# Seven products for the values of two dilated groups, tokens halved by residue, with evenly spread additions and transposed powers in the delta stage

## The chip, the cores and the metric

The kernel is one launch on one NeuronCore of a Trainium2 chip. The metric is device time in microseconds (us), the median of several executions. All matrices are float32. A float32 matmul shows in the profile as two MATMUL records, each with a LDWEIGHTS record of its own; a transpose through the identity matrix shows as one.

## The reference, cut to what matters

Two layers over 512 tokens of width 1024: an attention mixer with a mixture of experts, then a gated delta-rule mixer with a mixture of experts. Two places matter here.

- Attention: `qkv = h @ w_in` for three groups of 16 heads of 64 features. Group 0 attends to a window of 128 positions; groups 1 and 2 are dilated by 4, so that a query of residue r (its position modulo 4) sees only keys and values of residue r. q and k are rotated (`q * cos + swapped(q) * sin`), then come a softmax over all three groups together, the weighted sum of values, and the output projection.
- Delta rule: per head and per block of 128 tokens the inverse of a unit triangular matrix, `(I - A)^-1`, is needed.

## The kernel before

The program is a row of stages with a barrier of all engines between them: first (the modulated input `c.hT`, [128, 8 slices of the width, 512 tokens]), attention, experts, delta, experts.

**Attention.** Four turns (quads), of four heads each. A quad takes nine chunks of projection weights (256 features each, 1 MB) through a ring of three slots, in the order q0, k0, v0, q1, k1, q2, k2, v1, v2. SyncE (SP) asks for chunk n+3 as soon as chunk n is done with: after the halves of a q or k were swapped (`swapped`, L553), or after the value matmuls (`v_done`).

Each of the six q and k chunks (numbered s = 0 to 5) is projected by seven products in place of eight (`product_1` to `product_7`, Strassen's way in Winograd's form): features, the contraction and the tokens are halved, the tokens into the first 256 and the last 256 (`h11` to `h22`, L483). The weights stand still and 256 tokens move, so a product is 4 matmuls of 256 columns. Four of the products take token sums `t1` to `t4`, made once by VectorE in `c.x` at the start; the others take `h11`, `h21`, `h22` as they lie in `c.hT`. GpSimd makes four weight sums for each chunk (`add_up`, L694). Partial results are copied by ScalarE (`keep_m1`, `keep_u2`, `keep_u3`, `lay_21`, `keep_m5`) and joined by VectorE (`join`, L743), which lets TensorE overwrite the banks. VectorE then rotates (`rot`, `swp`) and writes q, k1 and k2 in the order of residues, through a strided output (L774, L778), k0 in the order of tokens (L776).

The values of group 0 are plain matmuls of 256 columns with 128 neighbouring tokens standing still (L912). The values of groups 1 and 2 (`PAIRED`, L907) go together: the 128 tokens of one residue stand still, `c.hT[:, kk, t:SEQ:RES]`, read with a step of four elements, and 512 features move, 256 of each group: 4 residues x 8 slices = 32 matmuls of 512 columns a quad. Four banks' worth of results are copied by ScalarE.

Beside this the stage builds the modulation rows for later (`AdaRows`): 24 weight tiles a quad, loaded by GpSimd's queue (L210, L213) into three slots and added up by VectorE (`ada.add`, L230). After chunk s's rotation begins, 2 additions are made, and after its end a further 2, 8, 2, 2, 0, 0 (`BETWEEN`, `BEHIND`, L541). The load of addition j waits for addition j-3, and GpSimd takes its work in order: the sums of chunk s+1, then the loads up to the additions behind chunk s. Matmuls with ones (`ada.total`, L246) and `ada.finish` (L255) end the rows. Behind the last value matmul TensorE starts the next quad's `product_1`; then scores, softmax, transposes and weighted values of the quad follow in eight steps.

**Delta.** Four turns of two heads. For each the powers of a nilpotent P and of its transpose Q are built (L2717 on): TensorE makes both P' = QP and Q' = PQ by four matmuls each (`each`, L2643), ScalarE copies both out (L2450, L2452), and `P E` is added to E by VectorE (L2620). Then three levels of links follow.

Of the kernel before, what the change touches and what calls it, by code (L numbers as in the profile page):

```python
# [274 lines left out]
def first_stage(nc, c, A, ring):  # L275
# [40 lines left out]
    with nc.Block() as block:  # L316
# [32 lines left out]
        def _(dve):  # L349
# [8 lines left out]
            ch.do(nc.vector.tensor_scalar(ang[:], pos[:], freq[:, 0:1], None, ALU.mult))  # L358
# [68 lines left out]
def attention_stage(nc, c, A, ada_rows, ring):  # L427
# [10 lines left out]
    VALS = 6  # L438
# [31 lines left out]
    ada = AdaRows(nc, c, st, A, (1, 2), ada_rows, 3, gate=True)  # L470
# [12 lines left out]
    h11, h12, h21, h22 = [c.hT[:, a * KH:(a + 1) * KH, b * SH:(b + 1) * SH] for a in range(2) for b in range(2)]  # L483
    toks = c.x[:].rearrange("p t n -> p (t n)").rearrange("p (m k s) -> p m k s", m=4, k=KH)
# [20 lines left out]

    sem = st.sem
    chain_done, second_done, third_done = sem("chain_done"), sem("second_done"), sem("third_done")
# [10 lines left out]
    VC = 2  # L518
# [22 lines left out]
    BETWEEN, BEHIND = 2, (2, 8, 2, 2, 0, 0)  # L541

    with nc.Block() as block:
        @block.sync
        def _(sp):
# [18 lines left out]
            def turn(i, following):  # L564
                ada.load_bias(sp, i)
                for n, (g, s) in enumerate(chunks):
                    if s < 2:
                        swapped(i, subs.index(n))
                    else:
                        sp.wait_ge(v_done, VALS * i + (2 if n < PAIRED else VALS))  # L570
# [23 lines left out]
        def _(act):  # L594
            act.sem_inc(chain_kept, 8)
            act.sem_inc(v_free, VC)
# [29 lines left out]
            def quad(i, following):  # L626
                b = 0
                for n, (g, s) in enumerate(chunks):
                    if s < 2:
# [8 lines left out]
                        continue  # L638
                    for _ in range(0 if n > PAIRED else 4 if n == PAIRED else 2):
                        act.wait_ge(v_done, VALS * i + b + 1)  # L640
                        bank = tp[b % 2][:].rearrange("p b q -> p (b q)").rearrange("p (a f) -> p a f", f=QF)
                        if n >= PAIRED:
                            nc.scalar.copy(v[:, 1:3, b - 2, :], bank).then_inc(v_free, 1)
                        else:
                            nc.scalar.copy(v[:, g, 2 * b:2 * b + 2, :], bank).then_inc(v_free, 1)
                        b += 1
# [45 lines left out]
        def _(pool):  # L692
# [16 lines left out]

            with pool.Fori(0, QUADS) as i:  # L710
                add_up(i, 0)
                j = 0
                for s in range(NSUB):
                    if s + 1 < NSUB:
                        add_up(i, s + 1)
                    for _ in range(min(BETWEEN + BEHIND[s] + (ada.slots if s == 0 else 0), ada.steps - j)):
                        ada.load(pool, i, j)
                        j += 1
                assert j == ada.steps

        @block.vector
        def _(dve):
# [17 lines left out]
            for i in range(QUADS):  # L740
# [12 lines left out]
                j = 0  # L753
                for s in range(NSUB):
# [7 lines left out]
                    for _ in range(min(BETWEEN, ada.steps - j)):  # L762
                        ada.add(dve, i, j)
                        j += 1
# [3 lines left out]
                    for pair in range(2):  # L768
                        if pair == 0:
                            ch.sync()  # L770
                        a = rot[:, pair].rearrange("p (j r) -> p j r", r=RES)
                        b = swp[:, pair].rearrange("p (j r) -> p j r", r=RES)
                        if keys == 0:
                            ins = nc.vector.tensor_tensor(q[:, g, pair].rearrange("p (r j) -> p j r", r=RES), a, b, ALU.add)  # L774
                        elif g == 0:
                            ins = nc.vector.tensor_tensor(k0[:, pair, P:P + SEQ], rot[:, pair], swp[:, pair], ALU.add)  # L776
                        else:
                            ins = nc.vector.tensor_tensor(k[:, g - 1, pair].rearrange("p (r j) -> p j r", r=RES), a, b, ALU.add)  # L778
                        ins.then_inc(rot_done, 1)
                    dve.wait_ge(rot_done, NROT * i + 2 * s + 4)  # L780
                    for _ in range(BEHIND[s]):
                        ada.add(dve, i, j)
                        j += 1
                assert j == ada.steps
                ada.finish(dve, i, 0, side, 1)
                ada.finish(dve, i, 2, gate_side, 2)
                ada.finish(dve, i, 1, side, 3)
# [34 lines left out]
        def _(pe):  # L822
# [7 lines left out]
            def times(out, left, right, kks, done, start=False):  # L830
                for kk in kks:
                    last = nc.tensor.matmul(out, left[:, kk], right[:, kk], start=start and kk == 0, stop=kk == KH - 1,
                                            skip_group_check=True)
                if kks[-1] == KH - 1:
                    last.then_inc(done, 1)

# [35 lines left out]
            def quad(i, following):  # L872
                b = 0
                for n, (g, s) in enumerate(chunks):
                    if s < 2:
                        u = subs.index(n)
                        if u == 0:
                            pe.wait_ge(sm_ready, UNITS * i + 2)
                            product_5(i, 0)
                            product_2(i, 0)  # L880
# [13 lines left out]
                    if n > PAIRED:  # L894
                        continue
                    pe.wait_ge(w_in[n % SLOTS], 16 * (CH // SLOTS) * i + 16 * (n // SLOTS + 1))
                    if n == PAIRED:
                        pe.wait_ge(w_in[(n + 1) % SLOTS], 16 * (CH // SLOTS) * i + 16 * ((n + 1) // SLOTS + 1))
                    else:
                        pe.wait_ge(pT_ready, UNITS * i + 2)  # L900
                    for _ in range(4 if n == PAIRED else 2):
                        pe.wait_ge(v_free, VALS * i + b + 1)
                        bank = tp[b % 2][:].rearrange("p b q -> p (b q)")
                        if n == PAIRED:
                            t = b - 2
                            for kk in range(KT):
                                last = nc.tensor.matmul(bank.rearrange("p (a f) -> p a f", f=QF), c.hT[:, kk, t:SEQ:RES],  # L907
                                                        w[:, PAIRED % SLOTS:PAIRED % SLOTS + 2, kk], start=kk == 0, stop=kk == KT - 1)
                        else:
                            for t in range(2 * b, 2 * b + 2):  # L910
                                for kk in range(KT):
                                    last = nc.tensor.matmul(bank[:, t % 2 * QF:(t % 2 + 1) * QF], c.hT[:, kk, t * P:(t + 1) * P],  # L912
                                                            w[:, n % SLOTS, kk], start=kk == 0, stop=kk == KT - 1)
                        last.then_inc(v_done, 1)
                        b += 1
                        if b == VALS - 2:
                            pe.wait_ge(ada.ready, ada.readies * i + 2)
                            ada.total(pe, i, 2, gate_side)
                pe.wait_ge(ada.ready, ada.readies * i + 3)
                ada.total(pe, i, 1, side)  # L920
                if following:
# [57 lines left out]
                for step in range(PAIRS + 3):  # L979
                    if step == 0:  # L980
                        pe.wait_ge(rot_done, NROT * (i + 1) + 2)
                        pe.wait_ge(ada.ready, ada.readies * (i + 1))
                        scores(0)
# [6 lines left out]
                    if step == 0:  # L990
                        pe.wait_ge(v_free, VALS * (i + 1) + VC)
# [9 lines left out]
            product_1(0, 0)  # L1001
            pe.wait_ge(toks_ready, 2)
            product_6(0, 0)
            pe.wait_ge(toks_ready, 4)
            product_7(0, 0)
# [1248 lines left out]
def delta_stage(nc, c, A, ada_rows, ring):  # L2254
# [75 lines left out]
    pw_ready = [sem(f"pw_ready{n}") for n in range(3)]  # L2330
    e_done = [sem(f"e_done{n}") for n in range(6)]
# [27 lines left out]
    with nc.Block() as block:  # L2359
# [24 lines left out]
        def _(act):  # L2384
# [23 lines left out]
            with act.Fori(0, TURNS) as i:  # L2408
# [36 lines left out]
                for s, (pd, qd) in enumerate(((P1, Q1), (P0, Q0), (P1, None))):  # L2445
                    for h in range(HP):
                        act.wait_ge(pw_done[s], 2 * i + h + 1)
                        if s == 1:
                            act.wait_ge(E_first, 2 * i + h + 1)
                        last = nc.scalar.copy(pd[h][:], ps[h][1][:])  # L2450
                        if qd is not None:
                            last = nc.scalar.copy(qd[h][:], ps[h][2][:])  # L2452
# [370 lines left out]
```

## Time and profile before

| | us |
|---|---|
| median of 3 runs (2622.71 to 2629.01) | 2624.84 |
| the profiled execution's own time | 2624.83 |
| its span, first to last instruction | 2623.1 |
| TensorE busy in the span | 2456.6 (94%) |
| VectorE, ScalarE, GpSimd busy | 1209.0, 588.0, 490.8 |

The mean granted clock of TensorE is 0.983 of full speed. TensorE is busy nearly everywhere, so the table says which engine to look at, not what a change is worth.

### The profile page before, as it was taken

To read this page: it belongs to the slowest core of one execution; us is meant where nothing else is said; L and a number is where in the kernel's file an instruction comes from. 1 tells how busy PE (TensorE), PEld (TensorE's weight loads), DVE (VectorE), ACT (ScalarE), POOL (GpSimd) and SP (SyncE) were. 2 spreads that over 40 slices of the span, in tenths; PEclk is the share of its full clock that TensorE was granted. 3 is DMA by queue.
4 is the path that set the end of the run, shared out by engine and by line. 5 is a ranking of instruction groups with operands and counts; after the bars stand their busy time and mean duration, and the time that the engine had idled before them with its cause. 6 is when DMAs were issued, how large, how long until landed. Compare 5 with 4: busy or idle time off the path is not lost. (4 is left out here: it accounts for less than half of the span.)

```text
span 2623.1 us, 38415 instructions
## 1 busy us (share of the span) xinstructions
PE 2456.6 (94%) x14213; PEld 1443.2 (55%) x14214; DVE 1209.0 (46%) x2562; ACT 588.0 (22%) x1357; POOL 490.8 (19%) x488
## 2 busy tenths in 40 slices
PE   5999999998999999999998999999899999999996
PEld 3878787776854333333334658576764433333332
DVE  3846566574444333332245544635443443333326
ACT  1131131413111111111113443334211111111111
POOL 2504224240001111111100212222001111111110
PEclk9999999999999999999998999999999999999998
DMA  7726354363468999999964131221629999999967
GB/s 255 208 72 193 113 153 121 106 184 119 194 231 331 388 421 418 410 420 398 418 252 169 52 91 53 68 72 40 232 102 340 364 418 420 402 420 414 396 272 292
DMA packets 173625, 657.36 MB, mean 251 GB/s; under 512 B 25300, under 2 KB 87100, under 8 KB 118296
## 3 DMA queue, kind: packets, MB, share of 16 engines
q1 hardware_dynamic: 117936, 409.57, 40.8%
q10 hardware_dynamic: 20280, 136.27, 12.9%
q0 software_dynamic: 35248, 109.36, 12.0%
q8 instruction: 103, 1.69, 0.3%
q14 instruction: 58, 0.48, 0.1%
HBM read 616.27 MB, written 53.52 MB: 255 GB/s over the span
## 5 line engine op out<-in xcount | busy, mean ns | idle before, releaser
L1724 DVE TENSOR_SCALAR core_oT<-moe_tx,moe_by,moe_plus 128x128 f32<-128x128 f32 x360 | 123.0, 404 | 543.8 <-PE moe_tx L1989 543.7
L2028 PE MATMUL moe_py<-weights_w,moe_hT 128*32 128x512 f32 (+2 forms) x1296 | 312.7, 596 | 0.9 <-ACT moe_hT L1444 0.9
L2014 PE MATMUL moe_ph<-weights_w,core_oT 128*32 128x512 f32 (+2 forms) x1216 | 303.6, 615 | 2.5 <-issue 2.5
L2014 PE MATMUL moe_pr<-weights_w,core_oT 128*64 128x512 f32 (+2 forms) x864 | 274.2, 601 | 10.5 <-DMA core_ring<-in_expert_w_dram 6.3
L1523 POOL DMA_INDIRECT y_rows<-moe_ysb,moe_yidx x90 | 102.2, 1136 | 929.7 <-DVE moe_idx L1716 563.1
L1444 ACT COPY moe_hT<-moe_th 128x256 f32<-128x256 f32 x90 | 33.6, 373 | 917.1 <-PE moe_th L1977 917.1
L2657 PE MATMUL gdn_pj<-core_hT,core_ring 128*128 128x512 f32 x512 | 226.3, 596 | 5.2 <-ACTq L2391 5.2
L2657 PEld LDWEIGHTS gdn_pj<-core_hT,core_ring 128*128 128x128 f32 x512 | 96.8, 191 | 122.1 <-issue 122.1
L2014 PEld LDWEIGHTS moe_pr<-weights_w,core_oT 128*64 128x64 f32 (+2 forms) x864 | 92.0, 141 | 125.5 <-issue 124.9
L2028 PEld LDWEIGHTS moe_py<-weights_w,moe_hT 128*32 128x32 f32 (+2 forms) x1296 | 92.4, 128 | 120.6 <-issue 113.3
L2028 PE MATMUL moe_py<-core_ring,moe_hT 128*32 128x512 f32 (+2 forms) x416 | 145.3, 596 | 2.6 <-DVE moe_ysb L1861 2.6
L2014 PE MATMUL moe_ph<-core_ring,core_oT 128*32 128x512 f32 (+2 forms) x512 | 145.0, 602 | 1.8 <-issue 1.8
L1416 ACT ACTIVATE core_oT<-moe_tx,moe_plus,moe_by 128x128 f32<-128x128 f32 x360 | 135.6, 456 | 46.8 <-PE moe_tx L1989 46.8
L1861 DVE SCALAR_TENSOR_TENSOR moe_ysb<-core_ada,moe_py 128x512 f32<-128x512 f32 x180 | 115.6, 683 | 54.5 <-PE moe_py L2028 54.0
L2014 PEld LDWEIGHTS moe_ph<-weights_w,core_oT 128*32 128x32 f32 (+2 forms) x1216 | 85.4, 121 | 93.4 <-issue 92.9
L2014 PE MATMUL moe_ph<-core_hT,core_oT 128*32 128x512 f32 (+1 forms) x416 | 127.2, 594 | 1.9 <-issue 1.9
L1519 POOL DMA_INDIRECT core_oT<-h_rows,moe_idx x90 | 91.4, 1015 | 135.7 <-DVE moe_yidx L1720 63.6
L907 PE MATMUL attn_tp<-core_ring,core_hT 128*128 128x512 f32 x256 | 111.2, 592 | 0.0
L2014 PE MATMUL moe_pr<-core_hT,core_oT 128*64 128x512 f32 (+2 forms) x224 | 99.1, 595 | 0.0
L1989 PE MATMUL moe_tx<-core_ident,core_oT 128*128 128x128 f32 x720 | 95.2, 275 | 0.0
L907 PEld LDWEIGHTS attn_tp<-core_ring,core_hT 128*128 128x128 f32 x256 | 78.6, 309 | 29.7
L2014 PE MATMUL moe_pr<-core_ring,core_oT 128*64 128x512 f32 (+1 forms) x192 | 89.8, 623 | 0.0
(455 smaller groups left out, 4173.4 us busy)
## 6 DMA issues: line engine op xcount, KB each, us to landing
weights_w<-in_expert_w_dram SPq DMA_DIRECT2D x160, 1024.0 KB, 14.9
weights_w<-in_expert_w_dram ACTq DMA_DIRECT2D x92, 1024.0 KB, 10.5
core_ring<-in_expert_w_dram SPq DMA_DIRECT2D x54, 1024.0 KB, 14.7
core_hT<-in_expert_w_dram SPq DMA_DIRECT2D x48, 1024.0 KB, 13.9
core_ring<-in_attn_w_in_dram SPq DMA_DIRECT2D x36, 1024.0 KB, 6.3
weights_w<-y_rows SPq DMA_DIRECT2D x32, 1024.0 KB, 13.3
core_ring<-in_expert_w_dram ACTq DMA_DIRECT2D x30, 1024.0 KB, 10.1
attn_ada_w<-in_ada_w_dram POOLq DMA_DIRECT2D x64, 384.0 KB, 4.2
```

What stands on the lines that cost most here:

```text
L907: last = nc.tensor.matmul(bank.rearrange("p (a f) -> p a f", f=QF), c.hT[:, kk, t:SEQ:RES], w[:, PAIRED % SLOTS:PAIRED % SLOTS + 2, kk], s ...
L1416: last = nc.scalar.activation(xT[:, b, k], tx[0][:, k], ACT.Identity, scale=by[:, k:k + 1], bias=plus[:, k:k + 1])
L1444: nc.scalar.copy(hT2[:, p % 2], th[:]).then_inc(hT_ready, 1)
L1519: pool.indirect_dma_start(xg[:, b], None, h_rows, bass.IndirectOffsetOnAxis(ap=idx[:, b:b + 1], axis=0), bounds_check=SEQ - 1, oob_is_err= ...
L1523: pool.indirect_dma_start(y_rows, bass.IndirectOffsetOnAxis(ap=yidx[:, s:s + 1], axis=0), ysb[:, b], None, bounds_check=SEQ * TOPK - 1, oo ...
L1724: last = nc.vector.tensor_scalar(xT[:, b, k], tx[1][:, k - 4], by[:, k:k + 1], plus[:, k:k + 1], ALU.mult, ALU.add)
L1861: return nc.vector.scalar_tensor_tensor(out=out, in0=c.ada[:, 2, at], scalar=1.0, in1=in_, op0=ALU.add, op1=ALU.mult)
L1989: last = nc.tensor.transpose(tx[n][:, k], xg[:, b, 4 * n + k::KT], c.ident[:])
L2014: last = nc.tensor.matmul(ph[p % 2][at, :], xT[:, p % 2, k, at], w13[ew.up_place(n)[0]][:, :, k], start=k == 0, stop=k == KT - 1)
L2028: last = nc.tensor.matmul(py[n][at, :], hT2[:, p % 2, k, at], w2[ew.down_place(m)[0]][:, k, half(n)], start=k == 0, stop=k == 1)
L2657: last = nc.tensor.matmul(pj[m % 2][:], w[:, slot, k, m % 2 * P:(m % 2 + 1) * P], c.hT[:, k], start=k == 0, stop=k == KT - 1)
```

## The change

- The tokens are halved by residue: `h11` to `h22` and the sums `t1` to `t4` are residues 0 and 1, or 2 and 3. A half of `c.hT` is thus read with a step of four elements. The rotation tables are built in residue order too.
- q, k1 and k2 are now written densely; k0 is written with a step.
- The values of groups 1 and 2 become seven products: tokens by residue, the contraction, and group 1 against group 2. A product is 2 residues x 4 slices = 8 matmuls with 128 tokens standing still and 256 features moving. Four new weight sums a quad, each [128, 1024], are made by GpSimd (`add_up_values`), behind the sums of the last q or k chunk.
- Each chunk has four additions, two between and two behind, with four slots; the loads behind chunk s go only as far as its additions between.
- At the very start `product_2` is put ahead of `product_6`, and `product_7` waits for three token sums, not four.
- In the delta stage Q' is no longer a product: P' is copied out and transposed.

```diff
-    h11, h12, h21, h22 = [c.hT[:, a * KH:(a + 1) * KH, b * SH:(b + 1) * SH] ...]
+    by_residue = c.hT[:].rearrange("p k (j r) -> p k r j", r=RES)
+    h11, h12, h21, h22 = [by_residue[:, a * KH:(a + 1) * KH, b * RES // 2:(b + 1) * RES // 2] ...]
...
+    v11, v12, v21, v22 = [w[:, v_slots[b], a * KH:(a + 1) * KH] for b in range(2) for a in range(2)]
-    BETWEEN, BEHIND = 2, (2, 8, 2, 2, 0, 0)
+    ADDS = ada.steps // NSUB
...  (GpSimd)
+            def add_up_values(i):
+                for n in (PAIRED, PAIRED + 1):
+                    pool.wait_ge(w_in[n % SLOTS], ...)
+                nc.gpsimd.tensor_tensor(vs1, v21, v22, ALU.add).then_inc(v_sums, 1)
+                nc.gpsimd.tensor_tensor(vs2, vs1, v11, ALU.subtract).then_inc(v_sums, 1)
+                nc.gpsimd.tensor_tensor(vs3, v11, v21, ALU.subtract).then_inc(v_sums, 1)
+                nc.gpsimd.tensor_tensor(vs4, v12, vs2, ALU.subtract).then_inc(v_sums, 1)
...
                 for s in range(NSUB):
                     if s + 1 < NSUB:
                         add_up(i, s + 1)
-                    for _ in range(min(BETWEEN + BEHIND[s] + (ada.slots if s == 0 else 0), ada.steps - j)):
+                    else:
+                        add_up_values(i)
+                    far = ADDS * s + ADDS // 2 + ada.slots
+                    for j in range(ada.slots if s == 0 else far - ADDS, min(far, ada.steps)):
                         ada.load(pool, i, j)
...  (VectorE, behind the six chunks)
                 ada.finish(dve, i, 0, side, 1)
+                nc.vector.tensor_tensor(v[:, 1, 0:2], v[:, 1, 0:2], v_second, ALU.add).then_inc(v_joined, 1)
+                ada.finish(dve, i, 1, side, 2)
+                nc.vector.tensor_tensor(v[:, 1, 2:4], v[:, 1, 2:4], v_third, ALU.add).then_inc(v_joined, 1)
+                nc.vector.tensor_tensor(v[:, 2, 2:4], v[:, 2, 2:4], v_m5, ALU.add).then_inc(v_joined, 1)
+                ada.finish(dve, i, 2, gate_side, 3)
...  (TensorE, in place of the paired values)
+            def v_times(out, left, right, done, start=False):
+                for t in range(2):
+                    for kk in range(KH):
+                        last = nc.tensor.matmul(out[:, t], left[:, kk, t], right[:, kk], ...)
+                v_times(v_chain, h11, v11, v_chain_done, start=True)
+                v_times(v_second, h21, v12, v_second_done, start=True)
+                pe.wait_ge(v_sums, SUMS * i + 2)
+                v_times(v_chain, t2, vs2, v_chain_done)
+                v_times(v_third, t1, vs1, v_third_done, start=True)
+                pe.wait_ge(ada.ready, ada.readies * i + 2)
+                ada.total(pe, i, 1, side)
+                v_times(v_chain, t3, vs3, v_chain_done)
+                v_times(v_third, h22, vs4, v_third_done)
+                v_times(v_chain, t4, v22, v_chain_done)
+                pe.wait_ge(ada.ready, ada.readies * i + 4)
+                ada.total(pe, i, 2, gate_side)
...  (delta stage, TensorE)
-                    each(ps[h][1], lambda t: Q0[h][:, t], lambda t: P0[h][:, t])
-                    each(ps[h][2], lambda t: P0[h][:, t], lambda t: Q0[h][:, t]).then_inc(pw_done[0], 1)
+                    each(ps[h][1], lambda t: Q0[h][:, t], lambda t: P0[h][:, t]).then_inc(pw_done[0], 1)
...
                         if s < 2:
-                            last = each(ps[h][1], lambda t: q[h][:, t], lambda t: p[h][:, t])
+                            turn(ps[h][2], p[h], q_done[s])
                         if s == 0:
-                            each(ps[h][2], lambda t: p[h][:, t], lambda t: q[h][:, t]).then_inc(pw_done[1], 1)
                             pe.wait_ge(qk_ready, n)
                         each(ps[h][0], lambda t: p[h][:, t], lambda t: e[h][:, t]).then_inc(e_done[s], 1)
+                    if s < 2:
+                        for h in range(HP):
+                            pe.wait_ge(q_ready[s], 2 * i + h + 1)
+                            each(ps[h][1], lambda t: q[h][:, t], lambda t: p[h][:, t]).then_inc(pw_done[s + 1], 1)
```

## Rows read from the trace of the kernel before

**Rows 1.** Windows: stretch, its length, busy us (records) per engine, clock, DMA.
```profile
42.00:650.00 608.00, 586.60 (x3688) 470.40 (x3688) 380.17 (x657) 149.79 (x369) 195.41 (x192) 1.00 0.46 140
1425.00:1534.00 109.00, 108.58 (x561) 73.89 (x560) 55.80 (x87) 43.49 (x79) 24.76 (x26) 1.00 0.25 75
```
**Rows 2.** Timeline of TensorE, second quad's values: start, us, record xcount.
```profile
286.90 13.90 PE L907 MATMUL attn_tp<-core_ring,core_hT 128*128 128x512 f32 x32
301.07 13.91 PE L907 MATMUL attn_tp<-core_ring,core_hT 128*128 128x512 f32 x32
221.31 13.98 PE L912 MATMUL attn_tp<-core_ring,core_hT 128*128 128x256 f32 x64
```
**Rows 3.** By line: duration of one, ns, least/median/most; 128x128 weight loads.
```profile
L907 PEld LDWEIGHTS attn_tp<-core_ring,core_hT x256: 307/308/328, 138.1 to 612.6; 128*128 128x128 f32 x128
L912 PEld LDWEIGHTS attn_tp<-core_ring,core_hT x256: 190/190/190, 72.3 to 530.8; 128*128 128x128 f32 x128
```
**Rows 4.** Timeline of TensorE in the delta stage, 128-column products and a transpose.
```profile
1485.67 1.06 PE L2646 MATMUL gdn_ps<-gdn_P,gdn_Q 128*128 128x128 f32 x8
1486.57 1.06 PE L2646 MATMUL gdn_ps<-gdn_Q,gdn_P 128*128 128x128 f32 x8
1500.18 0.60 PE L2651 MATMUL gdn_ps<-core_ident,gdn_E 128*128 128x128 f32 x4
1500.62 1.06 PE L2646 MATMUL gdn_ps<-gdn_E,gdn_P 128*128 128x128 f32 x8
```
**Rows 5.** Transposes whose input is read with a step: by line, and in the timeline.
```profile
L2087 PEld LDWEIGHTS moe_tx<-core_ident,core_x x64: 186/188/206, 673.7 to 1931.1; 128*128 128x128 f32 x64
673.95 1.05 PE L2087 MATMUL moe_tx<-core_ident,core_x 128*128 128x128 f32 x8
```
**Rows 6.** Timeline: matmuls whose moving operand is read in runs of four elements.
```profile
27.60 8.37 PE L405 MATMUL first_sums<-first_w,core_c 128*1 128x512 f32 x64
```
**Rows 7.** By line: the projection products that move `c.hT` itself.
```profile
L832 PE MATMUL attn_sc<-core_hT,core_ring x288: 379/379/483, 57.0 to 575.4; 128*128 128x256 f32 x144
L832 PE MATMUL attn_proj<-core_hT,core_ring x96: 379/379/763, 42.4 to 560.7; 128*128 128x256 f32 x96
L832 PE MATMUL attn_sc<-core_hT,attn_even_sums x96: 379/379/379, 58.7 to 570.3; 128*128 128x256 f32 x96
L832 PE MATMUL attn_sc<-core_hT,attn_prob x96: 379/379/379, 69.1 to 582.4; 128*128 128x256 f32 x96
```
**Rows 8.** Waits of TensorE, 42 to 615 us: us in total, times, longest.
```profile
PE attn_sc L832 <- POOL attn_prob L704: 4.3, 3, 2.0
PE attn_proj L832 <- POOL attn_even_sums L704: 2.9, 4, 0.9
PE attn_sc L832 <- DVE attn_raw L746: 1.2, 1, 1.2
```
**Rows 9.** Timelines of GpSimd and SyncE, first quad: loads, weight sums, a chunk's load.
```profile
99.68 0.54 POOL L213 DMA_DIRECT2D attn_ada_w<-in_ada_w_dram  x1 [0.93 <-DVE attn_ada_acc L230]
100.24 1.28 POOL L702 TENSOR_TENSOR attn_prob<-core_ring 128x512 f32<-128x512 f32 x1
129.02 0.62 SPq L551 DMA_DIRECT2D core_ring<-in_attn_w_in_dram  x1
146.08 1.27 POOL L702 TENSOR_TENSOR attn_even_sums<-core_ring 128x512 f32<-128x512 f32 x1 [15.48 <-DMA core_ring<-in_attn_w_in_dram]
```
**Rows 10.** DMA issues: KB each, median us to landing.
```profile
core_ring<-in_attn_w_in_dram SPq DMA_DIRECT2D x36, 1024.0 KB, 6.3
attn_ada_w<-in_ada_w_dram POOLq DMA_DIRECT2D x32, 128.0 KB, 2.4
```
**Rows 11.** VectorE: lines of 42 to 615 us (mean ns), and token sums of the start.
```profile
L774 DVE TENSOR_TENSOR attn_q<-attn_rot,attn_swp 128x512 f32<-128x512 f32 x24 | 23.5, 1057 | 0.4
L776 DVE TENSOR_TENSOR attn_k<-attn_rot,attn_swp 128x512 f32<-128x512 f32 x8 | 5.2, 688 | 0.1
48.65 2.28 DVE L734 TENSOR_TENSOR core_x<-core_hT,core_x 128x1024 f32<-128x1024 f32 x1
```

More of the change, by code:

```diff
@@ L779, in _ @@
                         ins.then_inc(rot_done, 1)
                     dve.wait_ge(rot_done, NROT * i + 2 * s + 4)
-                    for _ in range(BEHIND[s]):
+                    for j in range(ADDS * s + ADDS // 2, ADDS * (s + 1)):
                         ada.add(dve, i, j)
-                        j += 1
-                assert j == ada.steps
                 ada.finish(dve, i, 0, side, 1)
-                ada.finish(dve, i, 2, gate_side, 2)
-                ada.finish(dve, i, 1, side, 3)
+                dve.wait_ge(v_second_done, i + 1)
@@ L831, in times @@
                 for kk in kks:
-                    last = nc.tensor.matmul(out, left[:, kk], right[:, kk], start=start and kk == 0, stop=kk == KH - 1,
+                    last = nc.tensor.matmul(by_half(out), left[:, kk], right[:, kk], start=start and kk == 0, stop=kk == KH - 1,
                                             skip_group_check=True)
@@ L835, in times @@
                     last.then_inc(done, 1)
+            def v_times(out, left, right, done, start=False):
+                for t in range(2):
+                    for kk in range(KH):
+                        last = nc.tensor.matmul(out[:, t], left[:, kk, t], right[:, kk], start=start and t + kk == 0,
+                                                stop=kk == KH - 1, skip_group_check=True)
+                last.then_inc(done, 1)
             def product_1(i, s):
@@ L893, in quad @@
                         continue
-                    if n > PAIRED:
+                    if n >= PAIRED:
                         continue
                     pe.wait_ge(w_in[n % SLOTS], 16 * (CH // SLOTS) * i + 16 * (n // SLOTS + 1))
[L897 to L905, printed above, removed]
-                            for kk in range(KT):
[L907 to L913, printed above, removed]
-                        last.then_inc(v_done, 1)
[L915 to L918, printed above, removed]
@@ L919, in quad @@
-                pe.wait_ge(ada.ready, ada.readies * i + 3)
-                ada.total(pe, i, 1, side)
+                    pe.wait_ge(pT_ready, UNITS * i + 2)
+                    for half_ in range(2):
+                        bank = tp[half_][:].rearrange("p b q -> p (b q)")
+                        for t in range(2 * half_, 2 * half_ + 2):
+                            for kk in range(KT):
+                                last = nc.tensor.matmul(bank[:, t % 2 * QF:(t % 2 + 1) * QF], c.hT[:, kk, t * P:(t + 1) * P],
+                                                        w[:, n % SLOTS, kk], start=kk == 0, stop=kk == KT - 1)
+                        last.then_inc(v_done, 1)
```

118 lines of the change are left out of this document (79 added, 39 removed).

## The prediction

> **What bounds the kernel now.** First the windows by stage: in the attention stage TensorE is busy for 586.6 of 608 us, in one turn of the delta stage for 108.58 of 109 us, both at the full clock [rows 1]. In both stages the change touches TensorE's own work, so what counts is how long a record occupies TensorE, then what it waits for. Then the timelines: there the distance from start to start tells the occupation. A record of 512 columns takes (13.90 - 0.592)/31 = 0.429 us, one of 256 columns (13.98 - 0.379)/63 = 0.216 us [rows 2]. In the delta stage a set of four 128-column products starts 0.90 us after the last, a set of four transposes hands over after 0.44 us [rows 4]. Last the waits: in the attention stage TensorE's idle time in front of products is 4.3 + 2.9 us for GpSimd's weight sums and 1.2 us for a join, in 8 places [rows 8]. The stages end in barriers and nothing else overlaps the two, so what TensorE saves there, the span saves.
>
> **The values of two groups.** Before: 32 matmuls of 512 columns are 64 records x 0.429 = 27.5 us a quad. After: 7 products x 8 matmuls are 112 records of 256 columns x 0.216 = 24.2 us. That is 3.3 us a quad, 13.2 us over four.
>
> Against it stand the weight loads. Three of the seven products (h11, h21, h22) hold 128 tokens still that are read with a step of four elements: 48 records a quad. Such a load takes 308 ns where a dense one takes 190 [rows 3]. Behind a matmul of 0.429 us it was hidden. Now the cover is 0.216 us. Loads overlap one another: in the delta stage 128-column records follow at 0.112 us ((1.06 - 0.275)/7) [rows 4] though a dense load lasts some 190 ns. So a load's occupation is about 0.112 us dense, and with the step 0.112 + 0.118 = 0.230 us. Bounds: nothing (0.216 stays the limit), or the whole load exposed at 0.32 us, which is 192 x 0.104 = 20 us. I take 0.230: 192 x 0.015 = +3 us. Sum for the values: -13.2 + 3 = -10.2 us (between -13.2 and +6.8).
>
> **The projections: a moving operand with a step.** Products 1, 2 and 3 of every q and k chunk now move a half of `c.hT` with a step of four elements, 16 bytes: 288 + 96 + 96 + 96 = 576 records of 256 columns [rows 7]. No row of before shows a moving operand with such a step. Below: no cost. Above: the stationary load of the same `c.hT` with the same step slows by 118 ns over 128 elements [rows 3], 0.92 ns each, so 256 moving elements would take 0.236 us more, 576 x 0.236 = +136 us. Nearer the lower end lie two rows. Matmuls that move runs of four elements with four skipped keep (8.37 - 0.592)/63 = 0.123 us a record, four of them side by side in the array, so 0.49 us for four where dense ones of 512 columns take 0.429 [rows 6]. And transposes that load a stationary operand with a step of eight elements follow at (1.05 - 0.273)/7 = 0.111 us for 128 elements [rows 5], 0.87 ns per element fetched by itself. A float32 record moves a column in 0.216/256 = 0.84 ns. A fetch of one element a column is thus about as fast as needed, if each column is fetched once. I take nothing; the upper end is the first rival.
>
> The Trainium skill speaks against this edit ("SBUF — State Buffer", section on the 16-byte cachelines): accesses that each cross into a new 16-byte line pay a penalty, as a step of four float32 elements does. The stationary loads of L907 agree with it, 308 against 190 ns [rows 3]; whether the moving side does, no run here shows. By that rule the sum is the first rival's.
>
> **Stalls of the projections.** GpSimd works in order. Before, it issues the loads for the additions behind chunk s-1 ahead of the sums of chunk s+1, so these start late: at 99.68 us a load had waited for VectorE, and the sums of the next chunk began at 100.24 us, as that chunk did [rows 9]. After, the loads reach only to the additions between, and the sums start right behind them, half a chunk earlier. The 8 waits (8.4 us; 9.7 us with the 0.16 us by which the modelled ends of the matmuls overhang) should go [rows 8]. What is late next is VectorE's join: chunks s = 2 and 3 now have four additions of 768 columns each where they had two wide and two narrow. Writing q and k densely gives back 2 x (1.057 - 0.688) = 0.74 us a chunk [rows 11], and the bank that a join frees is needed only two products (3.4 us) later. I take -7.5 us (between -9.7 and 0).
>
> **New waits in the value part.** The second slot's weights are asked for at 129.02 us [rows 9] and land after about 6 us [rows 10], at 135. GpSimd's four sums are twice as wide as the 1.27 us ones [rows 9], so 2.5 us each, up to 3.4 when VectorE is busy: ready at 137.5, 140, 142.5, 145 to 148. TensorE starts the values at about 138.4 and wants the second at 138.4 + 2 x 3.45 = 145.3, the others later: hidden, with some 3 us to spare. But the loads of the last two additions now stand behind these sums in GpSimd's queue: issued at 146 to 149, landed 2.4 us and more later [rows 10], added by 150 to 153. `ada.finish` of the first row stands behind these additions on VectorE, and `ada.total` of the second row, in the middle of the products (at 138.4 + 4 x 3.45 = 152.2), waits for it, with three products queued behind it. That is 0 to 3 us a quad; I take 0.5, so +2 us. The copies and joins of the values (0.59 to 0.69 us each) have a whole product between them and their users.
>
> **The start.** The token sums take about 2.2 us each beside GpSimd's sums [rows 11], and TensorE waits for them. They now read with a step. VectorE's write with a step costs 1057 - 688 = 369 ns over 512 elements [rows 11]; the same for reading 1024 is +0.74 us each, +3 us at the fourth. Against that, `product_2` (1.7 us) fills a wait and `product_7` no longer waits for the fourth. Between -2.6 and +1; I take -1 us.
>
> **The delta stage.** A turn has 16 sets of products in the powers (4, 6, 4, 2). It will have 12, and 4 sets of transposes: 4 x 0.90 - 4 x 0.44 = 1.84 us less [rows 4], 7.4 us over four turns. The chain is longer, since Q' needs P' copied and transposed. Walked through for two heads: P' of head 0 ends at 0.90 us, is copied 0.75 us later, when the other head's P' is just made (1.80); each later copy (0.59 us and about 0.25 of hand-over) has at least 0.9 us of the other head's work above it. The tightest places have under 0.1 us to spare. Bounds -7.4 to -3; I take -7.3.
>
> **Sum.** -10.2 + 0 - 7.5 + 2 - 1 - 7.3 = -24.0 us, against the profiled execution's 2624.83 us, which is the median of the runs shown (2624.84): **2600.8 us**.
>
> **The rivals.**
> - *Slower: the moving step.* Place: products 1, 2, 3 of the projections. If the moving side pays as the stationary load does, 2600.8 + 136 = 2737 us; a few us of that would hide stalls. It decides from 24/576 = 0.042 us per record on: above that the change loses. For: the same tensor, the same step, slowed by 1.6 times in L907. Against: the two rates above, one of them with a greater step. A sixth: 0.16.
> - *The stationary step is not overlapped.* The three value products run at 0.32 us a record: +17 more, 2618 us. For: 308 ns is longer than the 216 ns cover. Against: loads overlap in the delta stage. 0.11.
> - *The stalls move.* The waits for sums go, but VectorE's joins, or the last additions (3 us a quad), come in their place: +10, 2611 us. For: GpSimd has 10 us more work a quad, and VectorE was waited for once already [rows 8]. Against: TensorE asks for them late. 0.08.
> - My forecast 0.63; something better than 2588 us 0.02.
>
> **The numbers.** My own case spans 2590 to 2610 (the bounds of stalls, start and loads partly offset). A range of 2588 to 2622 takes in the second and third rivals and leaves out the first and the tails, 0.2. Within 0.2% (5.2 us, about what a measurement of this kernel can tell from no change) is 2619.6 to 2630: it takes 0.03 of the second rival's and 0.02 of others. Faster 0.79, same 0.05, slower 0.16.
>
> **What would show it.** Records of L832 with `core_hT` moving still last 379 ns and follow at 0.216 us: the moving step is free; at 0.45 us the first rival is true. The value products with `core_hT` standing still follow at 0.23 us, those with `core_x` at 0.216. TensorE's waits for GpSimd's sums vanish from the attention stage, and a wait of about 0.5 us for `ada.finish` appears before L246. In the delta stage a turn is 1.8 us shorter with no new wait for ScalarE's copies. I am wrong if the attention stage has not shrunk by 15 us or more.

## The result, and the profile after

The changed kernel takes **2731.1 us** (median, 2730.61 to 2732.66 over four executions), the kernel before 2626.5 on the same chip: a ratio of **1.0395** (1.0381 to 1.0409), 3.95% slower. The forecast was 2600.8 us. What came is the first rival, the moving step, priced at 2737. Ratios compare executions in the usual state only: two among the experiments, of 5891 and 11125.57 us, were in a slower one and are left out.

The loss is in one stage. From TensorE's first projection record to its last record of the stage, attention took 606.5 us before and 718.8 after; the first mixture-of-experts stage 767.2 and 769.0, the delta stage 438.2 and 432.5. The spans of the two profiled executions differ by 2731.0 - 2623.1 = 107.9 us, the three stages by +112.3, +1.8 and -5.7.

Engines of the page after:
```profile
PE 2578.4 (94%) x14341; PEld 1463.2 (54%) x14342; DVE 1182.6 (43%) x2574; ACT 591.1 (22%) x1361; POOL 522.2 (19%) x504
```
TensorE is busy for 94% of the span again. Its 122 us of additional busy time look like work, though there are fewer columns to multiply. A busy share doesn't show that each record has become slower; the records grouped by line do (duration of one, ns, least/median/most):
```profile
L877 PE MATMUL attn_sc<-core_hT,core_ring x288: 610/629/632, 45.7 to 687.1; 128*128 128x256 f32 x144
L877 PE MATMUL attn_proj<-core_hT,core_ring x96: 611/629/769, 41.9 to 665.7; 128*128 128x256 f32 x96
L877 PE MATMUL attn_sc<-core_hT,attn_even_sums x96: 612/632/696, 58.4 to 678.1; 128*128 128x256 f32 x96
L877 PE MATMUL attn_sc<-core_x,attn_prob x192: 377/379/397, 69.3 to 690.8; 128*128 128x256 f32 x192
...
L885 PEld LDWEIGHTS attn_tp<-core_ring,core_hT x128: 308/329/332, 165.6 to 706.3; 128*128 128x128 f32 x128
```
The records that move `c.hT` last 629 ns where they lasted 379 [rows 7]; those that move a token sum out of `c.x`, of the same shape, stay at 379. The timeline shows the occupation (start, us, line, operation, records):
```profile
93.65 3.77 PE L877 MATMUL attn_proj<-core_hT,core_ring 128*128 128x256 f32 x8
97.25 3.79 PE L877 MATMUL attn_sc<-core_hT,core_ring 128*128 128x256 f32 x8
100.85 1.91 PE L877 MATMUL attn_proj<-core_x,attn_even_sums 128*128 128x256 f32 x8
102.60 1.89 PE L877 MATMUL attn_sc<-core_x,attn_even_sums 128*128 128x256 f32 x8
104.33 1.89 PE L877 MATMUL attn_proj<-core_x,core_ring 128*128 128x256 f32 x8
...
165.93 7.61 PE L885 MATMUL attn_tp<-core_ring,core_hT 128*128 128x256 f32 x32
173.38 3.62 PE L885 MATMUL attn_tp<-attn_probT,core_x 128*128 128x256 f32 x16
...
192.65 3.77 PE L877 MATMUL attn_proj<-core_hT,core_ring 128*128 128x256 f32 x8
```
From start to start a product of eight records takes 3.60 us with the step and 1.73 without: 0.450 and 0.216 us a record. Over 576 records that is 576 x 0.234 = +135 us. The values of two groups go from 165.93 to 192.65, 26.7 us; before they took 29.2 (286.90 to 316.11, from the stretch of [rows 2]). So do the other quads, but that the last one, with scores behind it, took 30.6 and now takes 27.5: 3 x 2.5 + 3.1 = 10.6 us less in all. Their strided records follow at (7.61 - 0.397)/31 = 0.233 us.

TensorE's waits from 42 to 720 us (engine, line, whom it waited for: us in total, times, longest):
```profile
PE attn_proj L877 <- ACTq L614: 5.0, 1, 5.0
PE attn_tp L1010 <- DVE attn_prob L854: 0.8, 3, 0.3
PE attn_proj L877 <- ACT attn_u L632: 0.6, 1, 0.6
PE attn_proj L877 <- issue: 0.5, 1, 0.5
```
All waits of [rows 8] are gone, and no new one above 0.6 us has come (the 5.0 us stand at the start of the stage, before as after). That proves less than it seems to: a chunk now lasts 5.6 us longer on TensorE, and every other engine has time.

In the delta stage:
```profile
1600.06 2.20 PE L2709 MATMUL gdn_ps<-gdn_P,gdn_Q 128*128 128x128 f32 x16
1602.10 0.60 PE L2714 MATMUL gdn_ps<-core_ident,gdn_P 128*128 128x128 f32 x4
1602.53 1.06 PE L2709 MATMUL gdn_ps<-gdn_E,gdn_P 128*128 128x128 f32 x8
1603.43 0.60 PE L2714 MATMUL gdn_ps<-core_ident,gdn_P 128*128 128x128 f32 x4
```
Transposes stand where products Q x P stood. The first of them follows the two products by 2.04 us, where two sets of four take 2 x 0.90.

### The profile page after: what moved, and what is told of

The parts are those of the page before. It is cut to its first block and busy times, and to the rows that moved or that the text cites. A ratio compares the mean times of both kernels' runs of the same rounds, so it can differ in the third digit from the quotient of the medians.

```text
span 2731.0 us, 38755 instructions
## 1 busy us (share of the span) xinstructions
PE 2578.4 (94%) x14341; PEld 1463.2 (54%) x14342; DVE 1182.6 (43%) x2574; ACT 591.1 (22%) x1361; POOL 522.2 (19%) x504
## 5 line engine op out<-in xcount | busy, mean ns | idle before, releaser
L2075 PE MATMUL moe_ph<-core_ring,core_oT 128*32 128x512 f32 (+2 forms) x512 | 150.9, 634 | 4.7 <-issue 4.7
L877 PE MATMUL attn_sc<-core_hT,core_ring 128*128 128x256 f32 x288 | 134.0, 629 | 0.0
L877 PEld LDWEIGHTS attn_sc<-core_hT,core_ring 128*128 128x128 f32 x288 | 59.8, 207 | 64.9 <-issue 63.8
```

Source lines behind the costliest of these rows:

```text
L877: last = nc.tensor.matmul(by_half(out), left[:, kk], right[:, kk], start=start and kk == 0, stop=kk == KH - 1, skip_group_check=True)
L2075: last = nc.tensor.matmul(ph[p % 2][at, :], xT[:, p % 2, k, at], w13[ew.up_place(n)[0]][:, :, k], start=k == 0, stop=k == KT - 1)
```

## The experiments

**One part at a time.** First the halving by residue alone, on the kernel before:
```diff
-    h11, h12, h21, h22 = [c.hT[:, a * KH:(a + 1) * KH, b * SH:(b + 1) * SH] for a in range(2) for b in range(2)]
+    by_residue = c.hT[:].rearrange("p k (j r) -> p k r j", r=RES)
+    h11, h12, h21, h22 = [by_residue[:, a * KH:(a + 1) * KH, b * RES // 2:(b + 1) * RES // 2] for a in range(2) for b in range(2)]
```


> The kernel before with one part of the change: the projections' tokens halved by residue, so that products 1, 2 and 3 move c.hT with a step of four elements, and q, k1, k2 written densely. Theory (the moving step alone costs 0.235 us in each of 576 records, as the trace of after has it): 135 us more than before, less 1 to 4 us of stalls for sums that the longer products hide, so 2755 to 2762 us. Rival (the step is slow only beside something else that the change brought, such as the value products or GpSimd's wider sums): the records stay under 0.3 us and the kernel under 2690 us.

2755.6 us, ratio 1.0481 (1.0463 to 1.0498); the attention stage 736.9 us, 130 more than before. The records are as slow as in the changed kernel:
```profile
L838 PE MATMUL attn_proj<-core_hT,core_ring x96: 611/629/771, 43.4 to 680.5; 128*128 128x256 f32 x96
```
The step alone makes the loss, and more than the whole change does; the other parts give some of it back.

Then the delta inverse alone:

> The kernel before with the delta stage's part alone. Theory: 16 sets of products become 12 and 4 sets of transposes, 1.84 us a turn, so 7.4 us less than before: 2619 us. Rival (the longer chain P' copied, transposed, copied gives part of it back): 2 to 4 us less, with waits of TensorE for ScalarE's copies in the powers.

2622.2 us, ratio 0.9974 (0.9960 to 0.9987). A turn takes 107.45 us instead of 109.07, 1.62 less, in this kernel as in the changed one. Its attention stage, which is that of the kernel before, took 610.1 us in the profiled execution, not 606.5: the granted clock was 0.93 in its last 51 us, where it was 1.00. The stage times here come from one execution each, and a difference of 3 or 4 us between two of them shows nothing by itself.

Then the additions alone, four a chunk with four slots:
```diff
-    BETWEEN, BEHIND = 2, (2, 8, 2, 2, 0, 0)
+    ADDS = ada.steps // NSUB
```


> The kernel before with four additions a chunk and four slots alone. Theory (the waits for GpSimd's sums come from loads that stand ahead of them in its queue): the 8 waits of the attention stage go, 7.5 to 9.7 us less than before: 2617 to 2619 us. Rival (VectorE's joins get late in the chunks with four wide additions): waits for L746 in their place and no more than 3 us less.

2643.8 us, ratio 1.0052 (1.0036 to 1.0069): this part, which I had down for -7.5 us, costs 14 by itself (by the ratio). Its waits, then GpSimd and VectorE at the same time:
```profile
PE attn_sc L828 <- DVE attn_raw L746: 18.2, 8, 3.9
```
```profile
103.43 1.27 POOL L702 TENSOR_TENSOR attn_even_sums<-core_ring 128x512 f32<-128x512 f32 x1
104.78 1.26 POOL L704 TENSOR_TENSOR attn_even_sums<-attn_even_sums,core_ring 128x512 f32<-128x512 f32 x1
106.01 1.27 POOL L705 TENSOR_TENSOR core_ring<-core_ring 128x512 f32<-128x512 f32 x1
107.23 1.71 POOL L707 TENSOR_TENSOR attn_even_sums<-core_ring,attn_even_sums 128x512 f32<-128x512 f32 x1
```
```profile
101.13 1.02 DVE L230 SCALAR_TENSOR_TENSOR attn_ada_acc<-attn_ada_w,core_c,attn_ada_acc 128x768 f32<-128x768 f32 x1
106.42 3.08 DVE L765 TENSOR_TENSOR attn_swp<-attn_swp,attn_w_sin 128x512 f32<-128x512 f32 x2 [4.27 <-DMA attn_swp<-attn_raw]
109.53 1.95 DVE L772 TENSOR_TENSOR attn_q<-attn_rot,attn_swp 128x512 f32<-128x512 f32 x2
```
The waits for sums have gone and waits for VectorE's join stand in their place: twice as much. GpSimd's third and fourth sums lie beside the two sine products, which take 3.08 us together, 1.54 each, where the line's mean before was 0.68. VectorE's chain from the swap's landing to the next join gets longer, and the join late. Before, the sums lay beside the cosine products, which took 2.03 us in place of 0.69, and one join was waited for, 1.2 us [rows 8].
```profile
100.04 2.03 DVE L759 TENSOR_TENSOR attn_rot<-attn_raw,attn_w_cos 128x512 f32<-128x512 f32 x1
```

**The same spread with the old place of the sums.** Still four additions a chunk, but the loads for the additions behind a chunk stand ahead of the next sums in GpSimd's queue again:
```diff
-                    far = ADDS * s + ADDS // 2 + ada.slots
+                    far = ADDS * (s + 1) + ada.slots
```


> The kernel before with four additions a chunk and four slots, as in the additions-only run, but GpSimd issues the loads for the additions behind a chunk ahead of the next sums again, so that the sums start later. Theory (the additions-only run lost because the early sums run beside VectorE's sine products, 3.1 to 3.4 us in place of 1.3): those products are back at 1.3 us, the waits for joins fall from 18 us to under 6, and the time to 2630 us or less. Rival (four wide additions in chunks 2 and 3 are too much for VectorE whatever GpSimd does): the waits for joins stay at 14 us or more, 2640 us or more.

2631.7 us, ratio 1.0011 (1.0001 to 1.0021). Its waits, and the sine products' line (busy us, mean ns, idle before):
```profile
PE attn_sc L828 <- POOL attn_prob L704: 7.2, 4, 2.0
PE attn_proj L828 <- POOL attn_even_sums L704: 6.5, 4, 2.0
```
```profile
L765 DVE TENSOR_TENSOR attn_swp<-attn_swp,attn_w_sin 128x512 f32<-128x512 f32 x48 | 31.0, 685 | 37.9 <-DMA attn_swp<-attn_raw 37.9
```
The time is 2 us above the 2630 that I had expected at most, but the sine products are at 685 ns, no join is waited for, and the sums are late again. So it is the place of the sums, not the number of additions, that slowed VectorE. By the two ratios it explains eleven of the fourteen us.

**What in the step costs.** The changed kernel with other patterns of the moving operand, each under a line of its own; the patterns read tokens that the products don't want, so the projections are not the reference's, and only their time is read.
```diff
-                times(chain(s), weights(s)[0], h11, ALL, chain_done, start=True)
+                (step_two, run_two_odd)[s % 2](chain(s), weights(s)[0], chain_done, True)
```


> The changed kernel with other moving patterns, each of 256 columns, in products 1, 2 and 3 (its projections are not the reference's): in even chunks a step of two elements, aligned pairs with two skipped (output hopping too), a step of eight; in odd chunks pairs that start at an odd element, aligned pairs with dense output, runs of four with four skipped. Dense is 0.216 us a record, a step of four 0.451. Theory A (what costs is a new 16-byte line at each element): a step of two 0.216 us, pairs 0.216 us, aligned or odd in the same line, a step of eight 0.45. Theory B (what costs is an element fetched without its neighbour): a step of two 0.45 us, aligned pairs 0.216, odd pairs between 0.216 and 0.45, a step of eight 0.45. Theory C (any gap costs): pairs cost too, and only runs of four are free.

```profile
88.22 1.98 PE L897 MATMUL attn_proj<-core_hT,core_ring 128*128 128x256 f32 x8
90.04 1.97 PE L907 MATMUL attn_sc<-core_hT,core_ring 128*128 128x256 f32 x8
91.85 1.89 PE L877 MATMUL attn_proj<-core_x,attn_even_sums 128*128 128x256 f32 x8
...
97.03 3.84 PE L902 MATMUL attn_sc<-core_hT,attn_even_sums 128*128 128x256 f32 x8
100.69 1.91 PE L877 MATMUL attn_proj<-core_x,core_ring 128*128 128x256 f32 x8
102.44 1.97 PE L917 MATMUL attn_sc<-core_hT,core_ring 128*128 128x256 f32 x8
104.25 1.97 PE L912 MATMUL attn_sc<-core_hT,core_ring 128*128 128x256 f32 x8
...
111.24 1.89 PE L922 MATMUL attn_sc<-core_hT,attn_prob 128*128 128x256 f32 x8
```
From start to start, a record: step of two elements (L897) 0.228 us; neighbouring pairs with four from pair to pair (L907, and L912 with a dense output) 0.226; pairs that begin at an odd element (L917) 0.226; runs of four with four skipped (L922) 0.216, as dense; step of eight (L902) 0.458; step of four, above, 0.450. The time doubles where each element lies in 16 bytes of its own, and hardly rises where 16 bytes give two; doubling the step from four to eight adds almost nothing. That is Theory A, but for the 5% or so that a step of two and the pairs cost. No pattern had neighbours on either side of a 16-byte border, so whether the border counts, or only a jump of 16 bytes at every element, is not shown. Whether the output hops in the accumulator makes no difference (L907 against L912). One execution took 2632.3 us.

**The cure.** The changed kernel, whose products 1, 2 and 3 move the same columns in another order: at each position both residues, neighbours in `c.hT`, and the output's view turned with them.
```diff
+                    if right is h11 or right is h21 or right is h22:
+                        moving, to = moving.rearrange("p r j -> p j r"), to.rearrange("p r j -> p j r")
```


> The changed kernel, but products 1, 2 and 3 move the same tokens in another order: position by position, and for each the two residues of the half, which are neighbours in c.hT, so that two elements of each 16-byte line are fetched one behind the other. Theory (the whole loss is the lone element a line): 576 records fall from 0.451 to 0.227 us, 129 us less than the changed kernel. With the shorter products the waits for VectorE's joins and for ada.finish come back, some 10 us, as in the additions-only run and the patterns run: 2612 to 2620 us. Rival (the forecast's other terms were right, only the moving step was wrong): 2602 us, without such waits.

2623.9 us, ratio 0.9986 (0.9976 to 0.9996): 107.2 us come off (2731.1 to 2623.9) with another order of reading, a little more than the loss.
```profile
L880 PE MATMUL attn_proj<-core_hT,core_ring x96: 385/388/766, 42.5 to 565.7; 128*128 128x256 f32 x96
```
It is 4 us above the range that I had expected. Now that the products are short, the rest of the change shows:
```profile
PE attn_sc L880 <- DVE attn_raw L785: 10.6, 5, 2.7
...
PE attn_sc L246 <- DVE attn_ada_row L255: 2.3, 3, 1.3
```
The join waits of the additions' kernel are back, and a wait before L246, which the slow products had hidden. And a long wait can cost more than itself. One of the five in the timeline, then the windows there (stretch, length, busy us of PE, PEld, DVE, ACT, POOL with instructions, granted clock, DMA share, GB/s):
```profile
278.54 3.08 PE L880 MATMUL attn_sc<-core_hT,core_ring 128*128 128x256 f32 x8 [2.45 <-DVE attn_raw L785]
281.42 4.29 PE L880 MATMUL attn_sc<-core_x,attn_prob 128*128 128x256 f32 x16
285.54 1.89 PE L880 MATMUL attn_sc<-core_x,core_ring 128*128 128x256 f32 x8
```
```profile
276.00:278.00 2.00, 0.09 (x1) 0.00 (x0) 1.89 (x2) 0.37 (x1) 0.25 (x1) 1.00 0.00 0
278.00:280.00 2.00, 1.46 (x5) 1.26 (x6) 1.90 (x6) 0.37 (x1) 0.84 (x2) 0.84 0.22 66
280.00:282.00 2.00, 2.00 (x6) 1.54 (x6) 1.29 (x3) 0.00 (x0) 0.47 (x1) 0.50 0.90 223
282.00:284.00 2.00, 2.00 (x9) 1.69 (x8) 0.21 (x1) 0.00 (x0) 0.60 (x2) 0.81 0.87 190
284.00:286.00 2.00, 2.00 (x11) 1.74 (x11) 1.97 (x4) 0.63 (x2) 0.00 (x0) 1.00 0.86 258
```
After 2.45 us of idleness the granted clock falls to 0.50 (1.2 GHz of 2.4) and is back at 1.00 by 284 us. The eight records take 2.88 us from start to start instead of 1.81, the next sixteen 4.12 instead of 3.45: 1.7 us on top of the 2.45, and the same by the clock: (0.16 + 0.50 + 0.19) x 2 us. The waits of 2.49 and 2.72 us at 127.79 and 429.72 us went the same way; but behind the other of 2.72, at 581.29 us, the clock stayed at 1.00, and so it did behind the eight waits of 1.2 to 2.0 us in the kernel with the old place of the sums.

**Two attempts at both.** The pairs, the additions spread as before with four slots, and product 5 put ahead of product 6, which reads the last of GpSimd's sums:
```diff
-                        product_6(i, u)
                         product_5(i, u)
+                        product_6(i, u)
```


> The pairs kernel with the additions and loads spread as before (2 between, 2, 8, 2, 2, 0, 0 behind), four slots, and product 5, which needs only the first weight sum, ahead of product 6 in chunks 1 to 5. Theory (even spreading moved GpSimd's sums from under the swap's transfer onto VectorE's sine products, and put loads behind the value sums): the waits for joins, for sums and for ada.finish all fall under 3 us in total, 2597 to 2605 us, better than both kernels. Rival (VectorE is late for another reason, such as the value sums' length): no better than the pairs kernel within 3 us.

2620.4 us, ratio 0.9972 (0.9960 to 0.9983), 15 us above the range. The waits for sums, joins and rows are gone, as expected; new ones have come:
```profile
PE attn_sc L883 <- ACT attn_u L627: 5.5, 12, 0.5
...
PE attn_proj L883 <- ACT attn_u L627: 3.7, 8, 0.5
```
That is my own reordering: product 7 now stands right behind the product whose chain ScalarE must copy first. Twenty waits of 0.46 us.

And the same with the values of groups 1 and 2 as before, 32 wide matmuls:

> The tuned kernel with the values of groups 1 and 2 as before, 32 matmuls of 512 columns (and the kernel's old order of products at the very start). Theory: the seven products are worth 10.2 us, so 10 to 12 us more than the tuned kernel. Rival (their strided loads, joins and sums eat the gain): within 4 us of the tuned kernel.

2635.7 us, ratio 1.0027 (1.0014 to 1.0039). The attention stage is 621.1 us against 607.2: the seven products of the values, with the new order of the start (TensorE's waits of 2.0 and 1.9 us for the token sums are in this kernel only), are worth 13.9 us. The two can be told apart in the traces. The stretches of the values are those of the changed kernel and of the kernel before, 10.6 us apart. The first values come 30.4 us after the first product with the new start, 35.9 with the plain one, where TensorE not only waits longer but stood at a mean clock of 0.55 from 42 to 59 us, against 0.81. The sum, 16.1, is above 13.9 mainly because the clock was lower at the end of the first kernel's stage (0.93 against 1.00 in its last 51 us).

**Without the reordering, and with earlier sums.** First the products in their old order; then also one load fewer ahead of each chunk's sums.
```diff
-                    for _ in range(min(BETWEEN + BEHIND[s] + (ada.slots if s == 0 else 0), ada.steps - j)):
+                    for _ in range(min(BETWEEN + BEHIND[s] + (ada.slots - 1 if s == 0 else 0), ada.steps - j)):
```


> The kernel with the pairs in products 1 to 3 (2623.9 us, ratio 0.9986), and the additions spread and loaded as before (2; 2, 8, 2, 2, 0, 0) with four slots. Products stay in the order 7, 6, 5. Theory: the even spread costs by join waits (10.6 us in that kernel) and ada.finish (2.3 us); both go, and the waits for GpSimd's sums of before (7.2 us in 7) may come back, as the loads for the additions behind a chunk stand ahead of the sums again. Attention stage 600 to 604 us, total 2613 to 2618 us. Rival: the kernel whose product 5 was put ahead of product 6 had the same stage but for its 20 waits for ScalarE; if those waits were not on the path, this one comes out at its 2620 us again.

> The same, with one load fewer issued ahead of each chunk's sums (three of the four slots ahead instead of four), so GpSimd's sums start beside the last addition of the chunk before instead of after it, yet behind the sine products. Theory: the waits for sums shrink from some 7 us to under 2 us and the sine products stay under 0.75 us each: attention stage 595 to 600 us, total 2607 to 2613 us, the fastest of all. Rival: sums that run beside the last addition or the join slow VectorE there as they slowed the sine products; then a join wait of some us takes the place of the sum waits and the time is that of the kernel beside it within 2 us.

2606.4 us, ratio 0.9921 (0.9906 to 0.9937), and 2604.8 us, ratio **0.9914** (0.9901 to 0.9928): both beat the kernel before, by 0.8 and 0.9%, and the changed one. The attention stage takes 593.8 and 590.7 us. Of waits for weight sums, joins and rows, the first kernel has only
```profile
PE attn_sc L883 <- POOL attn_prob L728: 1.6, 1, 1.6
```
and the second none. The first came out 7 to 12 us better than I expected, since I had counted the join waits at their own length, without what the clock takes after them (between 242 and 442 us it stood at a mean of 0.98 in the pairs' kernel, at 1.00 here), and had feared 7 us of waits for sums. The first also shows what product 5 ahead of product 6 had cost: 13.4 us of the stage, of which the twenty waits are 9.2 and a lower clock near the end of its stage (0.93 against 0.97) some 2.

The second came out 2 us below its range, with a stage 4 us shorter than expected, and one thing was wrong in its theory: the sine products take 0.86 us on average, not under 0.75. In the last chunk of each quad the two take 3.44 us beside GpSimd's wide sums for the values; in all others 1.29. There no projection is waiting for the next join, so nothing is lost. The 1.6 us between the two kernels are inside the intervals of both; each of the five executions of the second is below each one of the first, but about 1.5 us of the stages' difference is a lower clock at the end of the first. So which is faster is not settled; only the trace says that the last wait for sums has gone and that no join is waited for.

## Why the prediction was wrong

**The step that failed** is "The projections: a moving operand with a step", where I wrote "I take nothing". It measured +135 us, against an upper bound of +136. The bound was worked out from the stationary load of the same tensor at the same step, 0.92 ns an element more; the moving side paid 0.234/256 = 0.91 ns. The rule of the Trainium skill ("SBUF — State Buffer", on the 16-byte cachelines), which I cited as speaking against, described it rightly, and I let two other rows outweigh it. Both were misread. The matmuls of [rows 6] move whole runs of four, which fill a line each: L922 above shows that such a pattern costs nothing, so this row said nothing of lone elements. And the 0.111 us of [rows 5] is the spacing of transposes whose *still* operand is read with the step; I set it beside the 0.84 ns that a moving column takes and called a lone fetch "about as fast as needed". The load did slow, which I hadn't looked up. The same view of the kernel before, for transposes with a dense input:
```profile
L952 PEld LDWEIGHTS attn_tp<-core_ident,attn_prob x256: 137/141/144, 173.6 to 646.0; 128*128 128x128 f32 x128
```
141 ns dense against 188 at the step of eight [rows 5]: hidden behind the transposes, not absent. The moving side has nothing to hide behind. The row nearest in mechanism (same tensor, same step, each element alone in its line, 190 against 308 ns) was the one I kept as the far bound, with a chance of 0.16.

**The values**: predicted -10.2 us, measured -10.6, with the strided record at 0.233 us against 0.230. Right. The second rival, a load not overlapped (0.32 us), is refuted by the same number.

**The stalls of the projections**: predicted -7.5. The waits did vanish, as said, and this showed nothing, since the slow products gave cover. By itself this part cost +14 us. (In the changed kernel too, sine products lasted up to 1.77 us, where none before was above 0.69.) The argument saw GpSimd's sums start earlier and not what they would then lie beside: the sine products of VectorE, which slowed from 0.68 to 1.54 us. I had named the join as next in line and dismissed it by the time at which TensorE frees a bank. The third rival ("the stalls move"), at +10 us, was the better account, hidden beneath the first.

**The wait for the last additions**: predicted 0 to 3 us a quad. Not there after; 2.3 us in three once the products are short. The mechanism was right.

**The start**: predicted -1. The token sums slowed by about 0.7 us each, as I had put it (2.87, 2.89 and 3.05 us for the first three where they took 2.10, 2.17 and 2.28). The slow first products keep the rest from being read in the changed kernel; the waits for token sums are 3.9 us in the kernel with residues and the plain start and at most 1.6 in those with the new one. From the first product to the first values it is 30.1 us before, and 29.8 and 30.0 in the two last kernels. The two edits of the start were not parted.

**The delta stage**: predicted -7.3 us, -1.84 a turn; measured -1.62 a turn, 6.5 over four, and -5.7 to -5.9 over the stage, whose opening, which is not changed, took some 0.7 us longer in both traces. The 0.22 lacking a turn is about the one gap in the chain: the first transposes wait 2.04 - 1.80 = 0.24 us for P' to be copied. I had put the tightest places at under 0.1 us to spare; one was over by more than that.

**The sum.** The last kernel, which has all of the change but the slow pattern and the even spread, is 2628.0 - 2604.8 = 23.2 us faster than the kernel before; that this is near my -24.0 is luck. The stalls went by another spread than the one that I had priced, the pairs cost 576 x 0.010 = 6 us that I had not counted, and 3 to 4 us of the gain are assigned to nothing.

## What to carry to other kernels

A moving float32 operand read at a step of 16 bytes doubled the time of its matmul here (0.216 to 0.450 us), though the same step in a still operand nearly hid (0.233): order the access pattern so that neighbours are read together, even if the output must then be written hopping (0.226 us). When two rows of different likeness bound an unknown, weigh them by the mechanism that they share with the case, and compare a load's duration, not the spacing of records that may hide it. And before one engine's work is moved earlier, look at what the others do in that stretch.

## What the runs showed of the hardware

- Moving float32 columns: 0.216 us per 256 dense or in runs of four, 0.226 in pairs (that begin at an even or an odd element), 0.228 at a step of two, 0.450 at a step of four, 0.458 at a step of eight. The Trainium skill ("SBUF — State Buffer", on the 16-byte cachelines) gives the rule, a penalty where each access crosses into a new line, and the runs agree. It also gives four fp32 elements as how far one can stride for free; a step of four was not free here, 0.450 against 0.216.
- A stationary load of the same tensor at a step of four lasts 308 ns against 190, and the records follow at 0.233 us in place of 0.216.
- An output written into the accumulator in hopping pairs costs no more than a dense one: 0.226 us for both.
- Two products of 512 columns on VectorE take 3.08 us beside GpSimd's sums; their mean is 0.685 each where the sums come later. Beside sums of 1024 columns the two take 3.44.
- Behind an idle stretch of 2.45 us on TensorE its granted clock fell from 1.00 to 0.50, 1.7 us of lost time on top. It fell behind three of the four such stretches of that kernel (2.45 to 2.72 us), not behind the fourth.
